# Moving the 31-tap convolution, two transposes and the memory normalisation to later places in a two-layer block

## What is computed

```
for l in range(2):
    h = rmsnorm(x, norm_mix[l])
    p = h @ w_in[l] + b_in[l]            # six parts of 1024: m, z, a, g, s, t
    y_m = mlstm_branch(m, z, ...)        # conv of 4 taps, 4 heads, norm, gate by silu(z), @ w_down
    y_c = conformer_conv_branch(a, g):   # u = a * sigmoid(g)
                                         # u = causal depthwise conv of 31 taps (u)
                                         # silu(layernorm(u)) @ w_pw + b_pw
    merged = sigmoid(s) * y_m + sigmoid(t) * y_c
    x = x + merged @ w_out[l]
    x = x + cross_attention(rmsnorm(x), rmsnorm(mem), wq, wk, wv, wo)
    x = x + conv_ffn(rmsnorm(x), ...)
return rmsnorm(x, final_norm)
```

## Time and profile before

| | |
|---|---|
| median of 3 runs | 2995.84 us (2994.2 to 2996.22) |
| the profiled execution | 2996.22 us, of which the span of the trace is 2994.9 us |
| PE busy | 2698.1 us, 90% |
| DVE busy | 2219.9 us, 74% |
| ACT busy | 1512.0 us, 50% |
| granted TensorE clock, mean | 0.941 of full speed |

### The profile page before, as it was taken

How to read it: one execution, slowest core, us unless ns; L and a number is a source line. 1 busy time by engine, 2 the same in 40 slices (tenths; PEclk the granted TensorE clock), 3 DMA queues, 4 the chain that set the end, 5 groups by cost and what they waited for, 6 DMA issues and landing times. The chain is left out here.

```text
span 2994.9 us, 37425 instructions
## 1 busy us (share of the span) xinstructions
PE 2698.1 (90%) x15514; PEld 2363.5 (79%) x15514; DVE 2219.9 (74%) x2532; ACT 1512.0 (50%) x1547; POOL 30.1 (1%) x61
## 2 busy tenths in 40 slices
PE   2887987969999999999999689899899899998997
PEld 1777886857888888888888589878799798787897
DVE  4876765757888888888888679935477788644686
ACT  1423333526777777777777454334444554244443
POOL 0000000000000000000000000000000000000000
PEclk8878998969999999999999889999999999999999
DMA  7646863418999999999999633354354433363452
GB/s 245 218 159 239 316 246 113 141 42 326 354 360 351 354 354 345 359 351 353 354 347 358 210 99 102 110 175 163 106 175 169 155 127 113 113 211 99 141 193 96
DMA packets 368912, 662.13 MB, mean 221 GB/s; under 512 B 27707, under 2 KB 192095, under 8 KB 364511
## 3 DMA queue, kind: packets, MB, share of 16 engines
q1 hardware_dynamic: 351968, 656.23, 62.5%
q10 hardware_dynamic: 16767, 3.43, 0.6%
HBM read 657.78 MB, written 1.84 MB: 220 GB/s over the span
## 5 line engine op out<-in xcount | busy, mean ns | idle before, releaser
L385 DVE TENSOR_TENSOR LO<-RAW,HI 128x2048 fp32r<-128x2048 f32 (+2 forms) x413 | 935.2, 2270 | 369.3 <-ACT HI L376 368.8
L376 ACT ACTIVATE HI<-RAW 128x2048 fp32r<-128x2048 f32 (+2 forms) x413 | 780.9, 1897 | 421.7 <-PE PS L392 360.2
L390 PE MATMUL PS<-X1H,HI 128*128 128x256 f32 (+1 forms) x2128 | 614.3, 289 | 3.2 <-DVE LO L385 3.2
L391 PE MATMUL PS<-X1L,HI 128*128 128x256 f32 (+1 forms) x2128 | 607.5, 285 | 0.0
L392 PE MATMUL PS<-X1H,LO 128*128 128x256 f32 (+1 forms) x2128 | 606.8, 285 | 0.0
L390 PE MATMUL PS<-HI,X1H 128*128 128x512 f32 x1056 | 431.1, 408 | 2.8 <-DVE LO L385 1.6
L390 PEld LDWEIGHTS PS<-X1H,HI 128*128 128x128 f32 (+1 forms) x2128 | 412.5, 194 | 7.5 <-DVE LO L385 3.4
L391 PEld LDWEIGHTS PS<-X1L,HI 128*128 128x128 f32 (+1 forms) x2128 | 412.2, 194 | 2.5 <-issue 0.5
L392 PE MATMUL PS<-HI,X1L 128*128 128x512 f32 x1056 | 413.5, 392 | 0.0
L391 PE MATMUL PS<-LO,X1H 128*128 128x512 f32 x1056 | 412.9, 391 | 0.0
L392 PEld LDWEIGHTS PS<-X1H,LO 128*128 128x128 f32 (+1 forms) x2128 | 411.7, 193 | 0.8
(11 more groups left out here) (362 smaller groups left out, 3033.5 us busy)
## 6 DMA issues: line engine op xcount, KB each, us to landing
RAW<-in_w_in_dram SPq DMA_DIRECT2D x68, 1024.0 KB, 5.2
RAW<-in_expert_w_gate_dram SPq DMA_DIRECT2D x66, 1024.0 KB, 5.2
RAW<-in_expert_w_up_dram SPq DMA_DIRECT2D x64, 1024.0 KB, 5.2
RAW<-in_expert_w_down_dram SPq DMA_DIRECT2D x62, 1024.0 KB, 5.6
RAW<-in_ffn_w_up_dram SPq DMA_DIRECT2D x55, 1024.0 KB, 5.2
AR<-in_expert_w_down_dram SPq DMA_DIRECT2D x50, 1024.0 KB, 5.3
AR<-in_expert_w_up_dram SPq DMA_DIRECT2D x48, 1024.0 KB, 5.5
AR<-in_expert_w_gate_dram SPq DMA_DIRECT2D x46, 1024.0 KB, 5.3
```

Of the source, the lines that this page charges most:

```text
L376: a.activation(HI[:, n % NH, 0:size(i)], raw_at(i), ACT.Copy).then_inc(*hi.up(i))
L385: v.tensor_tensor(LO[:, m % NH, 0:n], raw_at(i), HI[:, m % NH, 0:n].bitcast(F32), ALU.subtract).then_inc(*lo.up(i))
L390: t.matmul(o, lh, rh, start=first, stop=False)
L391: t.matmul(o, lh, rl, start=False, stop=False)
```

## The change

It changes the order of work in the three lists, and no instruction is added or left out.

- TensorE: the heads' transposes come after in2s chunk 1 and not after chunk 2; MEM's transposes after mld chunk 1 and not before mld; `turn_conv(2)` and `(3)` after the four xv chunks and not before them; the transposes of UT after in2t chunk 1 and not between xv chunks 1 and 2.
- ScalarE: the same moves for what goes with these; the squares of MEM after the evictions of in2s; UT's silu after in2t chunk 1; `first_taps(0)` after the eviction of in2a chunk 1.
- VectorE: fewer taps in each place up to the heads, MEM's scaling after the heads' work and two `split_lo`; the taps left over after the last gate of YM, in portions of 52 and 18, 14, and the remainder, with one `split_lo` behind each of the last three; UT's normalisation behind that, with two `split_lo` before UT's last step.

```diff
--- before.py
+++ after.py
@@ pe_layer2
         chunk(f"in2{l}s", 1, X1H, X1L)
-        chunk(f"in2{l}s", 2, X1H, X1L)
         t.wait_ge(*act_two("den", l))
         t.wait_ge(*dve_two("heads", l))
         pe_to_fm(t, ("ht", l), HT, [2, 3])
+        chunk(f"in2{l}s", 2, X1H, X1L)
         chunk(f"in2{l}s", 3, X1H, X1L)
-        pe_to_fm(t, ("mem", l), MEM, [4, 5, 6, 7], lambda nb: dve_two("normed", nb, "mem", l))
         chunk(f"mld{l}", 0, X2H, X2L, first=ready("ht"))
         chunk(f"mld{l}", 1, X2H, X2L)
+        pe_to_fm(t, ("mem", l), MEM, [4, 5, 6, 7], lambda nb: dve_two("normed", nb, "mem", l))
...
-        for cp in range(4):
-            turn_conv(cp)
+        turn_conv(0)
+        turn_conv(1)
         for j, i in enumerate(CH[f"xv{l}"]):
-            if j == 2:
-                t.wait_ge(*dve_two("utn", l))
-                pe_to_fm(t, ("ut", l), UT, [2, 3])
...
-        for j in range(4):
-            chunk(f"in2{l}t", j, X1H, X1L)
+        turn_conv(2)
+        turn_conv(3)
+        chunk(f"in2{l}t", 0, X1H, X1L)
+        chunk(f"in2{l}t", 1, X1H, X1L)
+        t.wait_ge(*dve_two("utn", l))
+        pe_to_fm(t, ("ut", l), UT, [2, 3])
+        chunk(f"in2{l}t", 2, X1H, X1L)
+        chunk(f"in2{l}t", 3, X1H, X1L)
@@ act_layer2
+        ev_a(1)
         first_taps(0)
-        ev_a(1)
...
+        act_to_fm(a, ("ht", l), X2H, XC)
+        for j in range(2, 4):
+            ev_bias(f"in2{l}s", j, GS, ACT.Sigmoid, f"b_in{l}", 32)
+            split_hi(a)
         if l == 0:
             act_squares(a, MEM, lambda k, ns: MSQ[:, k, ns], lambda q: mem_in(l, 1), "mem")
-        ev_bias(f"in2{l}s", 2, GS, ACT.Sigmoid, f"b_in{l}", 32)
+        ev_copy(f"mld{l}", 0, YM, places[f"mld{l}", 0][0])
         split_hi(a)
-        act_to_fm(a, ("ht", l), X2H, XC)
-        ev_bias(f"in2{l}s", 3, GS, ACT.Sigmoid, f"b_in{l}", 32)
-        split_hi(a)
+        ev_copy(f"mld{l}", 1, YM, places[f"mld{l}", 1][0])
...
-        for cp in range(4):
-            ev_ut(cp)
-        act_fm_biased(a, ("ut", l), [2, 3], ACT.Silu, ...)
+        ev_ut(0)
+        ev_ut(1)
         for _ in range(3):
             split_hi(a)
...
         z.then_inc(*act_two.up("vm", l))
-        for j in range(4):
+        ev_ut(2)
+        ev_ut(3)
+        for j in range(2):
+            ev_bias(f"in2{l}t", j, GT, ACT.Sigmoid, f"b_in{l}", 40)
+            split_hi(a)
+        act_fm_biased(a, ("ut", l), [2, 3], ACT.Silu, ...)
+        for j in range(2, 4):
             ev_bias(f"in2{l}t", j, GT, ACT.Sigmoid, f"b_in{l}", 40)
             split_hi(a)
@@ dve_layer2: taps up to the heads, in order
-   20, 11, 11, 11, 12, 11, 25, 5, 3, 19, 3, 4, 6, 2, 6, 5, 4
+   9, 9, 9, 9, 10, 9, 14, 5, 3, 8, 4, 2, 4
...
         split_lo(v)
         conv_taps(4)
         split_lo(v)
-        v.wait_ge(*mem_in(l, 1))
-        if l == 0:
-            v.wait_ge(*pool_rs("rms", "mem"))
-        dve_scale(v, MEM, MEM, RSM, "mem", l)
         v.wait_ge(*act_two("skip", l))
...
         dve_lo_fm(v, ("ht", l), X2H, X2L, 3, XC)
-        split_lo(v)
-        conv_taps(16)
-        split_lo(v)
-        conv_taps(8)
+        for _ in range(2):
+            split_lo(v)
+        conv_taps(2)
+        v.wait_ge(*mem_in(l, 1))
+        if l == 0:
+            v.wait_ge(*pool_rs("rms", "mem"))
+        dve_scale(v, MEM, MEM, RSM, "mem", l)
...
         gate_ym(3)
-        conv_taps(240)
+        conv_taps(52)
+        for n in (18, 14, 240):
+            conv_taps(n)
+            split_lo(v)
...
         z.then_inc(*dve_two.up("utn", l))
+        split_lo(v)
+        split_lo(v)
         dve_fm_biased(v, ("ut", l), X2H, X2L, UC)
-        for _ in range(7):
-            split_lo(v)
+        split_lo(v)
+        split_lo(v)
```

More of the change, by code:

```diff
@@ L2282, in act_layer2 @@
             z.then_inc(*act_fm.up(("mem", l), cp))
-        for j in range(4):
+        for j in range(2, 4):
             ev_copy(f"mld{l}", j, YM, places[f"mld{l}", j][0])
-            if j == 0:
-                split_hi(a)
         def ev_ut(cp):
@@ L2295, in act_layer2 @@
         a.wait_ge(*dve_two("ymgate", 3, l))
-        for cp in range(4):
-            ev_ut(cp)
-        act_fm_biased(a, ("ut", l), [2, 3], ACT.Silu, lambda c: pcol(f"cv_ln_g{l}", c), lambda c: pcol(f"cv_ln_b{l}", c), UC)
+        ev_ut(0)
+        ev_ut(1)
         for _ in range(3):
@@ L2304, in act_layer2 @@
         z.then_inc(*act_two.up("vm", l))
-        for j in range(4):
+        ev_ut(2)
[3 more added lines that the diff above has]
+            split_hi(a)
+        act_fm_biased(a, ("ut", l), [2, 3], ACT.Silu, lambda c: pcol(f"cv_ln_g{l}", c), lambda c: pcol(f"cv_ln_b{l}", c), UC)
+        for j in range(2, 4):
             ev_bias(f"in2{l}t", j, GT, ACT.Sigmoid, f"b_in{l}", 40)
@@ L2408, in dve_layer2 @@
         split_lo(v)
-        conv_taps(20)
+        conv_taps(9)
         split_lo(v)
         glu(1)
-        conv_taps(11)
+        conv_taps(9)
         split_lo(v)
-        conv_taps(11)
+        conv_taps(9)
         split_lo(v)
-        conv_taps(11)
+        conv_taps(9)
         glu(2)
         split_lo(v)
-        conv_taps(12)
+        conv_taps(10)
         split_lo(v)
-        conv_taps(11)
+        conv_taps(9)
         glu(3)
         split_lo(v)
-        conv_taps(25)
+        conv_taps(14)
         v.wait_ge(*pe_two("gates", 1, 7, l))
@@ L2430, in dve_layer2 @@
                      between=(lambda: conv_taps(5), lambda: conv_taps(3)))
-        conv_taps(19)
+        conv_taps(8)
         v.wait_ge(*pe_two("cumsum", l))
@@ L2435, in dve_layer2 @@
         v.tensor_tensor(gates4(Gc), halves(GA)[:, :, 0:4], halves(CSF)[:, :, 4:8], ALU.add).then_inc(*dve_two.up("g", l))
-        conv_taps(3)
         split_lo(v)
@@ L2463, in dve_layer2 @@
                                    ALU.mult).then_inc(*dve_two.up("weights", h, l))
-        conv_taps(6)
         split_lo(v)
@@ L2493, in dve_layer2 @@
         z.then_inc(*dve_two.up("heads", l))
-        conv_taps(5)
         split_lo(v)
```

## The result

The changed kernel takes 3029.47 us (median of 4 runs, 3025.21 to 3032.14) against 2995.71 us before; the ratio is 1.0112, 95% interval 1.0095 to 1.013. It is slower, by 33.8 us, and the forecast was 3031. The profiled execution took 3029.71 us with a span of 3028.4 us.

A forecast was written before the change was run, and what follows sets the result against it. PE, busy 90% of the span, was taken to bound the kernel, so its waits count. Terms 6.7 + 16.8 + 6.6 - 0.8 + 6.0 = 35.3 us gave a forecast of 3031 us, range 3007 to 3043 us.

The forecast's parts named there:

- the most likely case: The whole forecast with all its terms holds: chance 0.70, its own range 3021 to 3042 us.
- three new or longer waits: PE's waits per layer: heads' transposes 10.1 us, VectorE's last tap 8.4 us, UT's transposes 5.6 us.
- Front taps at nothing: VectorE's taps before the heads: moving them away from the front costs nothing and gains nothing.
- The prediction's sign for it: Up to the end of in2s chunk 1 both traces agree within a microsecond; otherwise the early taps were misread.
- Heads one chunk earlier, 6.7 us: Heads' transposes after in2s chunk 1: waits 10.1 us against 7.6 and 5.9 us, costing 6.7 us over two layers.
- the rival of a faster kernel: VectorE takes up the heads at once, starting under 1.9 us after in2s chunk 1: 2988 us, chance 0.05.
- MEM later, hidden: MEM's later scaling ends before PE reaches its transposes after two mld chunks: hidden, with 3 us to spare.
- The last tap late, 16.8 us: At `turn_conv(3)` PE waits 8.4 us per layer for taps held behind in2t chunk 0's `split_lo`: 16.8 us.
- UT, 6.6 - 0.8 us: UT's transposes behind in2t chunk 1: waits 5.6 us instead of 2.3, costing 6.6 us; second pair's 0.4 us wait goes, -0.8.
- The clock, 6.0 us: Lower clock after new waits: 2.0 us behind the last tap, 1.0 behind UT per layer, 6.0 us; heads' loss unchanged.

The follow-up runs named there:

- heads and MEM: Kernel before with only the heads' transposes behind in2s chunk 1 and MEM's scaling and transposes later (24 taps go around MEM): 3003.38 us, ratio 1.0018.
- UT late: Kernel before with only UT's transposes and silu moved behind in2t chunk 1: 3005.69 us, ratio 1.0030.
- splits amid the taps: Changed kernel with all 114 left-over taps in one go and the three in2t splits behind them: 3009.57 us, ratio 1.0041.
- putting the taps back: Changed kernel with the tap counts of the kernel before up to the heads (158, not 95): 3010.91 us, ratio 1.0042.
- The heads' mend: Changed kernel with VectorE's low part of mld chunk 0 behind the heads' work, not in front: 3023.60 us, ratio 1.0096.
- silu first: Changed kernel with UT's silu ahead of the split of cvp chunk 0 on ScalarE: 3032.37 us; measured again, 3029.38 us beside 3029.56 us for the changed kernel.
- four banks: Changed kernel with taps in one go and PSUM banks 2 to 5 for the heads' and UT's transposes: 2969.32 us, ratio 0.9912.
- with two and with three mends: Changed kernel with taps in one go and heads before mld chunk 0's low part: 3003.09 us; with UT's silu before cvp chunk 0's split too: 3002.93 us.

## Why the prediction was right

The interval of the result lies inside the range of 3007 to 3043 us, and the most likely case came about: each of its three new or longer waits is there, with the length forecast to within 0.3 us. Measured alone, the parts cost 7.1 (heads and MEM), 9.4 (UT late) and 19.9 us (splits amid the taps), 36.4 us against 33.8 us together.

- **Front taps at nothing.** Right: the waits in front of the heads are those of the earlier trace rows, and putting the taps back changed nothing beyond 0.4 us a layer. The prediction's sign for it was that the traces agree within 1 us up to in2s chunk 1. Its eviction stands at 1890.31 against 1891.36, 1.05 us apart, but the second block had begun 1.10 us earlier in this execution (ScalarE's L494 at 1734.57 against 1735.67).
- **Heads one chunk earlier, 6.7 us.** Right: 10.1 us a layer as forecast, against 7.6 and 5.9 us; alone, this part cost 7.1 us. The point at which the rival of a faster kernel would decide was added up wrongly: its own terms, start + 3.76 - 1.03 + 2.3 us against 7.6 us, give a start 2.6 us after in2s chunk 1 in layer 0, and not 1.9. With the start at 2.2 us the wait measured 7.3 us.
- **MEM later, hidden.** Right: no wait of PE at its transposes appears.
- **The last tap late, 16.8 us.** Right: 8.2 and 8.1 us against 8.4 forecast. VectorE's idle time was 13.51 us against 13.4. Taking the splits out gave back 19.9 us, the waits and the slow chunks behind them.
- **UT, 6.6 - 0.8 us.** Right, a little large: step 2 waits 5.4 us and not 5.2, and the 0.4 us of step 3 are not there, since it found its bank free as soon as step 2 had ended, so (5.4 - 2.3 - 0.4) x 2 = 5.4 us against 5.8. Alone it cost 9.4 us with its clock. By the drain of about 1380 ns that the Trainium skill adds to a table switch (ScalarE: Activation LUTs, What ACT_TABLE_LOAD costs), the wait is estimated 1.4 us longer. The trace does not agree: silu begins 0.01 us after the load's 1.28 us (2022.68, 2023.97), and the measurement decides.
- **The clock, 6.0 us.** Right in sum, and partly by luck. The chunk behind the last tap took 2014.06 - 2006.91 = 7.15 us, 1.4 us above a full-clock chunk, and not 2.0; the one behind UT 1.1 us above it, as forecast with 1.0. But only chunks were counted, and the transposes in front of them run slower too: eight of UT's took 2.18 us, where 1.04 us is what eight take at full clock. And of the heads I had said that their loss stays the same; in layer 1 it grew by 0.8 us. The measured waits add up to 6.7 + 16.3 + 5.4 = 28.4 us. From PE's wait at L1973 to its first wait for L1921 the layers took 16.7 and 19.0 us longer than before, of which 13.4 and 15.0 us are waits, so some 7.4 us are left there for the clock, not 6.0. The span grew by 33.5 us, and the part of the program before the change was 1.1 us shorter in this execution, so 6.2 us are left over the whole: some 1.1 us came back in parts that the change does not touch, which no term of the prediction foresaw.

Two steps of my own experiments failed. The heads' mend was priced from the LO that it moved without the four taps and the LO still in front (7.3 us and not 6.2). And silu first was priced at 2 to 3 us by the wait that it removed; the wait went, and the times moved by less than the measurement can tell. It is the experiment that speaks against adding up waits: of a wait shorter by 1.8 us in front of a stretch at the lower clock about half was left directly behind it, and hardly anything a few waits on. Where the waits were removed altogether, as with four banks, the slow chunks went with them, and the gain was 40.2 us against the 37 us expected (2969.3 us measured, 2974 expected).

## What to carry to other kernels

- An instruction that waits for a transfer holds everything behind it in its engine's list. Before work is put behind such an instruction, follow its wait to the end: here LO, to HI, to the load, to the buffer's last reader. Independent work that has a due time goes in front of it.
- A move that shortens nothing has to be judged by what covers the wait at its new place. Both the heads and UT were moved from behind a chunk that covered VectorE's or ScalarE's preparation to a place where that preparation could only begin.
- If steps wait for each other's result only because they share two buffers, look for free buffers before looking for a better place. Four banks for four steps took away what no place did.

## What the runs showed of the hardware that was not expected

The granted clock does not follow a wait by its length alone. UT's wait of 2.3 us, 1.86 and 0.41 us, left it at 1.00 in the kernel before; the same wait in the kernel with the heads and MEM moved was followed by 3.4 us at 0.50, in both layers.

The low stretches of two kernels can lie at the same moments although their waits end 2 us apart: with two and with three mends the clock was at 0.50 from 2010.00 to 2016.70 and from 2074.90 to 2081.60 in both. The one that waited 5.38 us had 3.3 us of its following work at the lower level, the one that waited 3.58 us had 5.4 us, and the medians are 3003.09 and 3002.93 us.

And the 16 transposes in a row of the four-bank kernel in the changed order left no low stretch behind them. The heads' and UT's places of both layers ran at full clock throughout, while the changed kernel was at the lower level at each of its three waits:

```profile
1876.00:2058.00 182.00, 180.65 (x1152) 157.47 (x1150) 142.44 (x251) 78.38 (x110) 4.15 (x7) 1.00 0.50 163
2490.00:2676.00 186.00, 181.34 (x1155) 158.09 (x1153) 144.27 (x255) 77.30 (x105) 3.98 (x7) 1.00 0.50 164
```
